# Placement of split weights in SBUF, the fourth panel's split ahead of the norm, and a merge with two panels side by side

## The reference

```python
for i in range(4):                        # kinds: conv, attention, hyena, conv
    h = rmsnorm(x, norm_mix_g[i])
    x = x + mixer[i](h)                   # h @ w_in (1024 x 3072), a mixer, y @ w_out (1024 x 1024)
    x = x + swiglu(rmsnorm(x, norm_ffn_g[i]), f_w13[i], f_w2[i])   # 1024 x 5632, 2816 x 1024
h = concatenate([meta_tokens, x])         # 16 + 256 = 272 rows
u = _rmsnorm(h, norm_mix_w)
merged = sigmoid(a_gret) * y_ret + sigmoid(a_gmla) * y_mla         # retention and latent attention
h = h + merged @ w_o
h = h + _swiglu(_rmsnorm(h, norm_ffn_w), w_ffn_gate, w_ffn_up, w_ffn_down)
return _rmsnorm(h, norm_final_w)[:, 16:]
```

## Time and profile before

| | |
|---|---|
| runs, us | 1774.52, 1771.78, 1760.92 (median 1771.78) |
| profiled execution, us | 1752.1 |
| its span, us | 1750.3 |
| instructions | 37337 |
| mean granted TensorE clock | 0.991 |
| HBM read | 288.03 MB, 165 GB/s over the span |

### The profile page before, as it was taken

One profiled execution on the slowest core, in us unless ns is written; L12 is line 12 of the kernel. 1 busy time (PEld: TensorE's weight loads), 2 busy tenths in 40 slices (PEclk: granted clock), 3 DMA queues, 4 the chain that ended last, 5 costly groups with the idle time before them and its releaser, 6 DMA issues.

```text
span 1750.3 us, 37337 instructions
## 1 busy us (share of the span) xinstructions
PE 1691.5 (97%) x13776; PEld 1599.1 (91%) x13776; DVE 1227.7 (70%) x2013; ACT 971.9 (56%) x1352; POOL 12.9 (1%) x20
## 2 busy tenths in 40 slices
PE   7999999999999999999999999999999999999997
PEld 7999999888999987569999999999999876799997
DVE  6887766586777587888776678776566665577764
ACT  4467745365775454206774446775454645468742
POOL 0000200000000000000000000000000000000000
PEclk9999999999999999999999999999999999999999
DMA  6567674433766554105666456667454432256662
GB/s 206 167 206 240 192 230 139 160 109 97 252 198 223 164 166 141 64 1 158 204 199 213 158 170 183 205 193 250 154 180 145 137 140 61 73 165 198 194 225 70
DMA packets 79545, 290.15 MB, mean 166 GB/s; under 512 B 9739, under 2 KB 12140, under 8 KB 79340
## 3 DMA queue, kind: packets, MB, share of 16 engines
q1 hardware_dynamic: 79468, 289.11, 52.2%
HBM read 288.03 MB, written 1.05 MB: 165 GB/s over the span
## 4 chain that ended last, share of the span: by engine, by line
PE 84%; DVE 11%; ACT 2%; issue 2%; DVEq 0%; DMA 0%; SPq 0%; ACTq 0%
PE bank L570 24%; PE bank L572 23%; PE bank L571 23%; DVE wlo L1516 3%; PE bank L858 2%; PE bank L845 1%; PE bank L799 1%; DVE conv_cv L1625 1%; DVE rinv L1522 1%; PE bank L954 1%; DVE hy_z L1765 1%; PE bank L1050 1%; ACT whi L1148 1%; PE bank L1060 1%; PE bank L1023 1%
## 5 line engine op out<-in xcount | busy, mean ns | idle before, releaser
L1148 ACT CAST whi<-raw 128x1024 fp32r<-128x1024 f32 (+1 forms) x490 | 539.3, 1102 | 328.4 <-PE bank L572 293.0
L570 PE MATMUL bank<-xq_h,whi 128*128 128x256 f32 x2384 | 666.9, 280 | 8.2 <-DVE wlo L1516 8.1
L571 PE MATMUL bank<-xq_h,wlo 128*128 128x256 f32 x2384 | 660.4, 277 | 0.0
L572 PE MATMUL bank<-xq_l,whi 128*128 128x256 f32 x2384 | 660.4, 277 | 0.0
L1516 DVE TENSOR_TENSOR wlo<-raw,whi 128x1024 fp32r<-128x1024 f32 (+1 forms) x491 | 629.9, 1283 | 5.4 <-ACT whi L1148 2.7
L570 PEld LDWEIGHTS bank<-xq_h,whi 128*128 128x128 f32 x2384 | 448.2, 188 | 19.3 <-DVE wlo L1516 12.7
L571 PEld LDWEIGHTS bank<-xq_h,wlo 128*128 128x128 f32 x2384 | 447.8, 188 | 1.5 <-issue 1.5
L572 PEld LDWEIGHTS bank<-xq_l,whi 128*128 128x128 f32 x2384 | 449.1, 188 | 0.0
L570 PE MATMUL bank<-ffn_hh,whi 128*128 128x256 f32 x880 | 242.9, 276 | 0.0
L571 PE MATMUL bank<-ffn_hh,wlo 128*128 128x256 f32 x880 | 242.9, 276 | 0.0
L572 PE MATMUL bank<-ffn_hl,whi 128*128 128x256 f32 x880 | 242.9, 276 | 0.0
(11 more groups left out here) (336 smaller groups left out, 2365.0 us busy)
## 6 DMA issues: line engine op xcount, KB each, us to landing
raw<-in_w SPq DMA_DIRECT2D x414, 512.0 KB, 3.6
raw<-in_w SPq DMA_DIRECT2D x80, 704.0 KB, 4.2
att_bias<-in_bias SPq DMA_DIRECT2D x4, 512.0 KB, 5.7
hy_w<-in_filt_w SPq DMA_DIRECT2D x8, 256.0 KB, 5.4
hy_decay<-in_decay SPq DMA_DIRECT2D x4, 512.0 KB, 4.4
mla_uq<-in_uq SPq DMA_DIRECT2D x1, 1152.0 KB, 5.4
x<-in_xT SPq DMA_DIRECT2D x1, 1024.0 KB, 5.9
out<-x SPq DMA_DIRECT2D x8, 128.0 KB, 2.0
```

Of the source, the lines that this page charges most:

```text
L570: pe.matmul(ps, whi[:, slot, wc], hi[:, k, cols], start=first, stop=False)
L571: pe.matmul(ps, wlo[:, slot, wc], hi[:, k, cols], start=False, stop=False)
L572: mm = pe.matmul(ps, whi[:, slot, wc], lo[:, k, cols], start=False, stop=last)
L1148: nc.scalar.copy(slices(whi, p % RING, k, to), raw_slices(p % RING, k, to)).then_inc(panel_hi, 1)
```

## The change

Three parts.

1. **Placement.** `whi` and `wlo` become views into tensors that are four elements (16 bytes) longer and start behind those; 56 elements (`align_weights`) stand between them; `XROW_AT` goes from 48 to 24, `align_rows` from 16 to 56 elements, `L_FIRST` from {256: 32, 272: 16} to {256: 56, 272: 40}.
2. **The fourth panel.** `norm_inv` gets the phase that follows and does `split_lo` of its fourth panel first. It is given in nine places: in front of in1, in2, in3, up0 to up3, in_ret and up4. The steps of these phases leave it out at j = 0 (`split_early=1`, which takes the first round of four out of the loop).
3. **The merge.** TensorE's w_o runs through `merged`: panels 0 and 1 side by side, both for each merged row as it comes, then panels 2 to 7. VectorE's split behind the last mla_out panel comes behind the last two `yl2` rather than in front of them.

```diff
-XROW_AT = 48
+W_AT = 4
+XROW_AT = 24
-L_FIRST = {SEQ: 2 * META, L: META}
+L_FIRST = {SEQ: 56, L: 40}
-    whi = sb("whi", [P, RING, SLOT], F32R)
-    wlo = sb("wlo", [P, RING, SLOT], F32R)
+    def weight_ring(name):
+        flat = sb(name, [P, W_AT + RING * SLOT], F32R)
+        return flat[:, W_AT:].rearrange("p (r s) -> p r s", r=RING)
+    whi = weight_ring("whi")
+    sb("align_weights", [P, 56])
+    wlo = weight_ring("wlo")
-    sb("align_rows", [P, 16])
+    sb("align_rows", [P, 56])
+        def merged():
+            ph = PH["w_o"]
+            for j in range(2):
+                pe.wait_ge(panel_lo, ph.p0 + j + 1)
+                pe.wait_ge(bank_free, ph.t0 + j + 1)
+            for k in range(K8):
+                pe.wait_ge(y_lo, YBASE["mrg"] + k + 1)
+                for j in range(2):
+                    slot = (ph.p0 + j) % RING
+                    ps = bank[(ph.b0 + j) % 4][:, Q]
+                    wc = slice(k * P, (k + 1) * P)
+                    pe.matmul(ps, whi[:, slot, wc], mg["yh2"][:, k, Q], start=k == 0, stop=False)
+                    pe.matmul(ps, wlo[:, slot, wc], mg["yh2"][:, k, Q], start=False, stop=False)
+                    mm = pe.matmul(ps, whi[:, slot, wc], mg["yl2"][:, k, Q], start=False, stop=k == K8 - 1)
+                    if k == K8 - 1:
+                        mm.then_inc(panel_used, 1)
+            for j in range(2, 8):
+                panel(ph, j // 4, j % 4, mg["yh2"], mg["yl2"], Q, None)
-        product("w_o", mg["yh2"], mg["yl2"], Q, (y_lo, YBASE["mrg"]))
+        merged()
...
+        def split_fourth(ph):
+            split_lo(ph, 0, 0, 0, ph.k)
-        def norm_inv(norm, cols):
+        def norm_inv(norm, cols, ph=None):
+            if ph is not None:
+                split_fourth(ph)
             dve.wait_ge(root_ready, norm + 1)
...
-            split_lo(ph_mo, 0, 0, j, K8)
+            if j < 3:
+                split_lo(ph_mo, 0, 0, j, K8)
             for u in range(2):
...
                 V.tensor_tensor(mg["yl2"][:, m, Q], hid[:, u, Q], mg["yh2"][:, m, Q].bitcast(F32),
                                 ALU.subtract).then_inc(y_lo, 1)
+        split_lo(ph_mo, 0, 0, 3, K8)
```

More of the change, by code:

```diff
@@ L1106, in _, with steps @@
         assert norm + 1 == NORMS
-    def steps(eng, ph, first, n, step, chain=None, per=0, ahead=4, loop=True):
+    def steps(eng, ph, first, n, step, chain=None, per=0, ahead=4, loop=True, split_early=0):
         crossing = first + n == ph.n and ph.next_k != ph.k
         rounds = n // 4 - (1 if crossing else 0)
+        alone = 0
         def one(i, j, split):
             step(i, j, split)
-        if rounds > 1 and loop:
-            start = chain.n if chain else 0
-            with eng.Fori(0, rounds) as i:
+        if split_early:
+            for j in range(4):
+                one(0, j, None if j < split_early else ph.k)
+            alone = 1
+        if rounds - alone > 1 and loop:
+            start = chain.n - alone * per if chain else 0
+            with eng.Fori(alone, rounds) as i:
                 if chain:
@@ L1125, in steps @@
         else:
-            for i in range(rounds):
+            for i in range(alone, rounds):
                 for j in range(4):
@@ L1498, in _, with dve_steps @@
         mask_bias()
-    def dve_steps(*args):
-        steps(nc.vector, *args, ahead=3)
+    def dve_steps(*args, **early):
+        steps(nc.vector, *args, ahead=3, **early)
     @block.vector
@@ L1602, in step @@
                     low(i, 1)
-            dve_steps(ph, 0, ph.n, step)
+            dve_steps(ph, 0, ph.n, step, split_early=1)
         def short_conv(layer):
@@ L1607, in short_conv @@
             link(V.memset(cm["cu"][:], 0.0))
-            dve_steps(ph, 0, 8, scaled(ph, 0, 8, lambda j, m: cm["c"][:, m, :]))
+            dve_steps(ph, 0, 8, scaled(ph, 0, 8, lambda j, m: cm["c"][:, m, :]),
+                      split_early=1 if layer else 0)
             if layer == 0:
@@ L1719, in attention @@
                 evict(m, (ph.b0 + m) % 4)
-                split_lo(ph, 0, 0, m, K8)
+                if m:
+                    split_lo(ph, 0, 0, m, K8)
                 if m == 10:
@@ L1818, in multiply @@
                     dve.wait_ge(hs["Y"], 2 * n + f + 1)
-            dve_steps(ph, 0, 4, conv_step, link, 8)
+            dve_steps(ph, 0, 4, conv_step, link, 8, split_early=1)
             for p in range(4, 24):
@@ L1870, in decay_product @@
                 V.tensor_tensor(decay_of(h), decay_of(h), rx["e2"][:, h % 2, :], ALU.mult).then_inc(re["E"], 1)
-            dve_steps(ph, 0, 4, scaled(ph, 0, 4, lambda j, m: rt["t"][:, m, A]))
+            dve_steps(ph, 0, 4, scaled(ph, 0, 4, lambda j, m: rt["t"][:, m, A]), split_early=1)
             dve.wait_ge(re["lg"], 1)
@@ L2045, in _ @@
                 wing_weights(0)
-            norm_inv(norm, A)
+            norm_inv(norm, A, PH[f"in{layer}"] if layer else None)
             norm += 1
@@ L2056, in _ @@
             residual(PH[f"out{layer}"], ("ffn_g", layer * C), A, norm, A)
-            norm_inv(norm, A)
+            norm_inv(norm, A, PH[f"up{layer}"])
             norm += 1
@@ L2062, in _ @@
                      B if last else A)
-        norm_inv(norm, B)
+        norm_inv(norm, B, PH["in_ret"])
         norm += 1
@@ L2082, in _ @@
                                 ALU.subtract).then_inc(y_lo, 1)
+        split_lo(ph_mo, 0, 0, 3, K8)
         residual(PH["w_o"], ("ffn_w2", 0), A, norm, A)
-        norm_inv(norm, A)
+        norm_inv(norm, A, PH["up4"])
         norm += 1
```

## The result

| | before | after |
|---|---|---|
| runs, us | 1774.52, 1771.78, 1760.92, 1756.25 | 1794.71 to 1800.5 (4 runs) |
| median, us | 1766.35 | 1797.06 |
| profiled execution, us (span) | 1752.1 (1750.3) | 1795.7 (1793.9) |
| mean granted TensorE clock | 0.991 | 0.990 |

The changed kernel takes 1.0178 times as long, with a 95% interval of 1.0114 to 1.0242. The forecast was 1742 us, faster; the upper end of its range, 1786, is also passed. The fourth panels' splits and the merge did in the main what the prediction said of them; the placement did the opposite.

The account below looks back on a forecast made before the run. TensorE bounds it, through matmul pitch, idle gaps and half-clock stretches. Profiled 1752.1 - 7.3 - 3.3 - 4.5 = 1737.0 us, plus a quarter of a possible 19.7 us offset: 1742; own range 1730 to 1757, whole range 1722 to 1786.

Parts of the forecast that it names:

- What bounds the kernel: TensorE, busy 97%: only matmul pitch (levels 113.3 and 117.8 ns), idle gaps and half-clock stretches can move the time.
- Part 1: Splitting the fourth weight panel before the norm removes TensorE's waits for it: 7.3 us saved, bounds 0 to 8.3.
- Rival (d): The wait in front of panel 3 moves to panel 4: 1749 us; chance 0.12.
- Part 2: In w_o, two panels' work per merged row removes waits and a half-clock stretch: 3.3 us saved, bounds 1.8 and 3.3.
- Part 3: New start addresses of weights and rows make all matmuls fast: 4.5 us saved; all slow would cost 45 us.
- rival (b): The new distance of rows and weights makes the slow matmul level the rule: 1786 us; chance 0.15.
- (a): Placement changes nothing; lost gaps no longer end slow long stretches: 1762 us, or 1775 with all five slow; chance 0.22.
- (c): The fast level itself falls, fp32r matmuls reaching the transposes' 109 ns: 50 us saved, 1692 us; chance 0.06.
- The interaction: With the gap gone, the level found behind `total` is kept for 1535 matmuls: 6.8 us each time it is slow.
- The offset of 19.7 us: Runs above profiled time: if fixed, 1757 us; if slow long stretches, 1737; a quarter of it taken, giving 1742.

Follow-up runs that it names:

- e2: The changed kernel with the old addresses, so only the fourth panels' splits and the merge: 1762.06 us, 1.0008 times before.
- e3: The kernel before with only the fourth panels split ahead of the norm, old merge and addresses, one run: 1781.16 us.
- e11: The same kernel as e3, timed over ten runs: 1762.94 us, 1.0004 times before.
- e10: e6 plus the merge side by side, without the splits ahead of the norm: 1746.65 us, 0.992 times before.
- e5: The changed kernel with rows at 80 and weights at 144 (modulo 256), distance 64, odd rows: 1738.77 us, 0.9841 times before.
- e6: The kernel before with rows at 80 and weights at 144, without the splits or the merge: 1750.27 us, 0.9905 times before.
- e1: The kernel before with the new placement alone: 1805.08 us, 1.0268 times before.
- e9: Separate scan kernel: rows/weights 64/128, 0/144 and 80/144, each entered four ways; 64/128 slow in 7, 3, 20 and 0 of 21 (ones, short wait, long wait, nothing).
- e7: The changed kernel with both starts 16 bytes further on, rows 16 and weights 160, distance 144: 1740.33 us, 0.9849 times before.
- e4: Separate scan kernel, no other engine working: 256 pairs of starts, 36 matmuls each behind a matmul of ones; pitches from 113.3 to 123.3 ns.
- e8: The scan of e4 in shuffled order without the ones-matmul; distance 64 at 113.3 ns, distance 144 at 113.3 for odd rows and 120.0 for even.

## Why the prediction was wrong, step by step

**What bounds the kernel: right.** TensorE's pitch, gaps and half-clock stretches account for the result. The two levels of 113.3 and 117.8 ns at the old placement, and that a whole stretch keeps one, were read rightly; e2, e3, e11 and the scans show them.

**Part 1: right.** Seven of the eight waits are gone and the split lies in the idle time of the root. 7.3 us were forecast; the medians of e10 and e5 give 7.9, the waits in their traces 7.5. Rival (d), the wait at panel 4, came in hyena alone, as the prediction had it: 0.36 us in the changed kernel, 0.80 in e5.

**Part 2: right where the old wait costs clock.** 3.3 us forecast, 3.6 measured (e6 to e10). TensorE idles behind mla_out for 1.75 us in e10 and 2.11 in e5, where I had worked out 1.7, and it cost no clock. But the size hangs on the half-clock stretch that the old merge brings with it. From mla_out's last matmul to w_o's last it takes 26.8 us before and 23.5 in e2, 3.3 less; 28.0 in e6 and 23.8 in e10, 4.2 less; but 25.4 in e1, where the clock did not fall, and 23.9 in the changed kernel, 1.5 less.

**Part 3: this step failed.** I bounded the placement between "all fast", -4.5 us, and "all slow", +45, and took the fast end "because over 80% of the matmuls are there already and every stretch of over 400 is". That share was measured at distance 64, and it says nothing of distance 144, of which, as I wrote, no matmul of the trace had a price. The one row that spoke of other positions, in_ret's 115.2 ns, was slower than 113.3; it was the nearest row to a changed position and pointed away from the end that I took. The term was about +45 us by e1, 49.5 from where I put it, and the cause is pitch: 55.7 us in e1, of which 10 came back in waits and half-clock stretches. With a placement that is at 113.3 ns throughout, the rest of the sum stands: e5's profiled run is 1738.84 us where the prediction had 1737.0. The fast end itself was put too high: e6, the kernel before at such a placement, has 1750.58 profiled against 1752.1, a gain of 1.5 us and not 4.5.

The upper bound was too low as well. It supposed that a slow stretch is at 117.8 ns. The new placement has levels of its own, 116.7, 118.3 and 120.0, and the prediction named a third pitch as what would fell every figure of part 3. They differ between executions too: the last long stretch is at 118.3 ns in the changed kernel and at 116.7 in e1. With a mean of 118.92 against 117.8, 12,216 x 1.1 = 13.7 us come on top of rival (b)'s 1786: 1799.7, against 1795.7 profiled.

**The rivals.** (b) is the mechanism that came true, with a wrong size. (a) is refuted for the placement: it is far from neutral, and the Trainium skill (SBUF — State Buffer, "Who interferes with whom"), by whose rule TensorE never waits on anyone, gives no hint of it. Here the measurement decides: the scans have 113.3 to 123.3 ns with no other engine at work. But (a) was right on the other half: with the gap gone the levels at distance 64 stay a draw, and e2's median is 1762.06 where I had put 1762; that it fits to 0.1 us is luck, since the runs lie between 1751.8 and 1785.9. Its "all five, 1775" is what the profiled execution shows, 1774.91. (c) falls: no pair of starts goes below 113.3 ns in the scans or the kernels. Its price was too high besides: the earlier trace rows give 0.33 / 3 = 0.110 us, 3.3 ns under 113.3, which is 40 us and not 50. The 109.2 ns that the Trainium skill gives for 256 columns (TensorE: Matmul & The Clock Gate, "Back-to-back issue gap") was not seen in any fp32r stretch. The section gives it for an isolated matmul and says that in a stream of weight loads and matmuls both set the spacing; such a stream is what this kernel has, so the prediction was wrong to read (c) out of it.

**The interaction: right, and under-used.** I wrote that a level found behind `total` is kept for 1535 matmuls, but charged it only to the rival. At the old placement it takes back all that the moves give (e2, e11). In the three profiled executions without the fourth panels' waits (e2, e3, e11) 13 of 15 long stretches are at 117.8 ns to their end; in the one of before, with the waits, none of five is. Since before's median lies 8 to 14 us above that execution, slow stretches presumably come about there too, only fewer; how many, no trace shows.

**The offset of 19.7 us** between the profiled execution and the median was most likely drawn levels, and no fixed cost: with odd rows the profiled run lies within 1 us of the median (e5 1738.84 and 1738.77), and the runs of e5 lie within 7 us, where those of before beside it span 25.

**What stays open.** Why distance 64, and 144 with odd rows, give 113.3 ns and the rest don't, is not shown; the scans give the table, not its cause. Nor is it shown what at an entry decides the level of 64/128; the kind of entry and the stretch before it both have a say in e9, where a wait of 0.85 us led to 117.8 in 20 of 21, while the longer waits of the kernel before were followed by 113.3 in most stretches. Starts that aren't multiples of 16 were not tried.

## What to carry to other kernels

Treat the start addresses of moving rows and weights as a tuning size of their own: read the pitch from the counts in a window without pauses, and price a new pair of starts with a short scan before it goes into the kernel. Don't take a pair for good because one profile shows it fast: where one profile holds two levels for the same matmuls, and the runs spread widely (here 0.9 to 1.4% for the kernel before, against 0.1 to 0.4% in e5, e6, e7 and e10), look for a pair that has only one. And where a wait is removed, ask what state the wait used to end.

## What the runs showed of the hardware that I had not expected

- With 256 columns, a load of weights for each matmul and the clock at 1.00, the pitch is 113.3 ns at rows/weights distances of 64 and, for odd rows, of 144 bytes modulo 256, and 116.4 to 123.3 at nearly all others (e4, e8): up to 9%, with no other engine at work.
- Moving both starts by 16 bytes, at a distance kept at 144, took 56.7 us of 1797 (e7 against the changed kernel).
- Rows at an even multiple of 16 and distance 64 have two stable levels, 113.3 and 117.8 ns; at odd multiples only the faster, after some slower matmuls behind an entry. At 64/128 the level behind a matmul of ones followed the stretch that ran before it, in 20 of 20 (e9).
- Behind the same wait of some 2.42 us in the merge the granted clock stayed at 0.50 for 3.1 us in one kernel, for 5.5, 6.0 and 5.7 us in others (e3, e11, e6), and in e1, where no shorter wait came ahead of it, it stayed at 1.00.
